# Differential attention: the second map's scaling on GpSimd, difference and transposes one unit later, scores over each map's own 64 partitions

## The chip, the cores and the metric

The kernel runs on 1 core of one Trainium2 chip. The metric is the time of one execution in device microseconds (us); smaller is better. The engines of the core are called here as the profile calls them: PE (TensorE, matmuls; PEld its weight loads), DVE (VectorE), ACT (ScalarE), POOL (GpSimd) and SP (SyncE, which here only issues DMAs).

## The reference, cut to what matters

The kernel computes one inference step of a two-layer trunk with 128 context tokens and 512 latent tokens side by side (640 in all, D_MODEL 1024). Each layer has three token mixers on one input projection (an mLSTM, a latent attention called MLA, and the differential attention), a gated merge of the three and a squared-ReLU MLP. The change is in the differential attention, which has 4 heads with two softmax maps each:

```
q_d = dq.reshape(B, N, H_D, 2, DK_D)          # DK_D = 64, two maps side by side: 128 values a head
k_all, v_all = concat(cache, own)             # latent queries: 128 cached + 512 own keys
def one(qbs):
    p = probs(qbs[0], k)                      # softmax of the first map
    p = p - lam * probs(qbs[1], k2)           # minus lambda times softmax of the second
    return einsum("bhqk,bkhe->bqhe", p, v)
```

## The kernel before, in words

All five engines have a program written out by hand, in fixed order, and they meet at semaphores. Weights come from HBM in 512 KB blocks through a ring of four buffers (SP issues them). POOL splits each block into a rounded part `w_hi` and a remainder `w_lo` (L427, L430), 144 blocks a layer, and PE does three matmuls for each product (L459, L462, L463 in `project`). There are two slots for split blocks, so POOL may split a block only when PE has begun the block before it (`block_used`, L426).

The differential attention stands in each layer between the projections `dq`, `dk`, `dv` and the merge of the MLA branch (`merge_a`). Its input is `q_d` and `k_d` [128 partitions, head, token]: on partitions 0 to 63 lies the head's first map, on 64 to 127 the second. So that a matmul over all 128 partitions gives one map's scores alone, DVE lays out `q_map`: two buffers (in `stage` and `sq`), each with two copies of a head's queries, in which the other map's 64 partitions are zero (memsets L1712, copies L1718 in `lay_out`).

The work of the stage is 20 **units** a layer: 4 heads, and in each 4 tiles of 128 latent queries (640 keys: a *full* unit) and at last the 128 context queries (128 keys: a *late* unit, `LATE`). The functions called `attend` (one on each engine) go through them in a software pipeline. For unit i:

- PE `scores` (L614): for each of the two maps m one PSUM buffer of two banks (`big`, alternating), each of two matmuls with 320 columns (a late unit: one of 128). The trace has two records for every such fp32 matmul, so 8 for a full unit, 2 x 1 x 2 for a late one.
- DVE `maxes` (L1356): the negated row maximum of each map, read from PSUM.
- ACT `exps` (L968): exp with the row sum, from PSUM into `prob_tile`; that frees the PSUM buffer for map m of unit i+1.
- DVE `normalise`: reciprocal of the two row sums (L1364), second map times its factor and -lambda (L1371), then first map times its factor plus the second (L1373); this releases `p_ready`.
- PE `turn` (L628): 5 transposes into the one PSUM tensor `two`; ACT `copyT` (L978) copies them to SBUF; PE `values` (L645, L643): 10 records that multiply with the values. DVE `outputs` (L1382) copies a finished head from PSUM.

The order on PE in step i is scores(i+1), turn(i-1), values(i-2); on DVE maxes(i+1), normalise(i), outputs; on ACT exps(i+1), copyT(i-1). Three pairs of probability tiles are used in turn (`prob_tile`, L349): two in `prob_d`, the third in `t1` and `rs`. The MLA attention uses the same functions with one map and two heads side by side. POOL has nothing to do in the stage: it has split the first block of `merge_a` and waits for PE to begin it.

Of the kernel before, what the change touches and what calls it, by code (L numbers as in the profile page):

```python
# [23 lines left out]
CTX, LAT, PAST = 128, 512, 128  # L24
# [4 lines left out]
P = 128  # L29
# [113 lines left out]
NEG = -1e30  # L143

# [33 lines left out]
def trunk(nc, xT, condT, consts, small_d, past_d, first_d, w_d, yT, o_ckv, o_kr, o_dk, o_dv, o_C, o_m):  # L178
# [3 lines left out]
    with ctx:  # L182
# [39 lines left out]
        q_map = [stage, sq]  # L222
# [64 lines left out]
        neg_max, row_sum = cols[:, 12:16], cols[:, 16:20]  # L287
# [11 lines left out]
        q_map_ready = sem("q_map_ready")  # L299
# [21 lines left out]
        qnope_copied, v_copied = sem("qnope_copied"), sem("v_copied")  # L321
        maxed, exped, p_ready = sem("maxed"), sem("exped"), sem("p_ready")
# [25 lines left out]
        GROUPS = [(0, 0, CTX), (1, CTX, T)]  # L348
        def prob_tile(prob, maps, i, m):  # L349

            return prob[:, maps * (i % 3) + m, :] if i % 3 < 2 else (t1, rs)[m]
# [37 lines left out]
        def _(pool):  # L389
# [45 lines left out]
        def _(pe):  # L435
# [162 lines left out]
            def attend(l, name, maps, side, unit0, set0, q_of, k_of, v_of, heads, prob, probT, beside=None):  # L598
# [3 lines left out]
                def scores(i):  # L602
# [3 lines left out]
                    if maps == 2 and t == 0:  # L606
                        pe.wait_ge(q_map_ready, l * H_D + h + 1)
# [42 lines left out]
                for i in range(-1, n + 2):  # L650
                    if i + 1 < n:
                        scores(i + 1)
                    if beside and 0 <= i:
                        beside(i)
                    if 0 <= i - 1 < n:
                        turn(i - 1)
                    if 0 <= i - 2 and (i - 2) % side == side - 1:
                        if beside and i % 10 == 1:
                            pe.wait_ge(mod_kept, l * MOD_CHUNKS + 3 + (i - 11) // 10)
                        values((i - 2) // side)  # L660

            pe.wait_ge(started, 1)
            for l in range(DEPTH):
# [190 lines left out]
                attend(l, "da", 2, 1, 40, 4, lambda h, m: q_map[h % 2][:, m, :], lambda h, m: k_d[:, h, :],  # L854
# [30 lines left out]
        def _(act):  # L885
# [65 lines left out]
            def attend(l, name, maps, side, unit0, set0, heads, prob, probT, exp0, beside=None):  # L951
                units = attention_units(heads, side)

                def exps(i):
                    h, t = units[i]
                    if i >= 3:
                        act.wait_ge(pT_ready, l * 60 + unit0 + i - 2)
                    for m in range(maps):
                        use = USE[name][maps * i + m]
                        ps, b, _ = buf(use)  # L960
                        col = 2 * (i % 2) + m
# [20 lines left out]
                for i in range(-1, n + 1):  # L982
                    if i >= 1 and maps == 1:
                        copyT(i - 1)
                    if i + 1 < n:
                        exps(i + 1)
                    if i >= 1 and maps == 2:
                        copyT(i - 1)
                    if beside and i >= 0:
                        beside(i)  # L990
# [316 lines left out]
        def _(dve):  # L1307
# [37 lines left out]
            def attend(l, name, maps, side, unit0, set0, heads, prob, exp0, out, lay_out=None, beside=None):  # L1345
                units = attention_units(heads, side)

                def maxes(i):
                    h, t = units[i]
                    for m in range(maps):  # L1350
# [3 lines left out]
                        col = 2 * (i % 2) + m  # L1354
# [4 lines left out]
                def normalise(i):  # L1359
                    h, t = units[i]  # L1360
                    n = CTX if t == LATE else T
                    c0 = 2 * (i % 2)
# [23 lines left out]
                for i in range(-1, n + 3):  # L1386
                    if i + 1 < n:
                        maxes(i + 1)
                        h, t = units[i + 1]
# [4 lines left out]
                    if i >= side + 2 and i % side == 0:  # L1394
                        outputs((i - side - 2) // side)
# [87 lines left out]
            for l in range(DEPTH):  # L1483
# [203 lines left out]
                attend(l, "ma", 1, 2, 0, 0, H_A, prob_a, 0, o_a, None, mods_beside(l))  # L1687
# [21 lines left out]
                for tile in q_map:  # L1709
                    for m in range(2):  # L1710
                        other = 64 * (1 - m)
                        v.memset(tile[other:other + 64, m, :], 0.0)  # L1712

                def lay_out(h):

                    for m in range(2):
                        r = slice(64 * m, 64 * m + 64)
                        v.tensor_copy(q_map[h % 2][r, m, :], q_d[r, h, :])  # L1718
                    dve.drain().then_inc(q_map_ready, 1)
                lay_out(0)  # L1720
                lay_out(1)
# [3 lines left out]
                attend(l, "da", 2, 1, 40, 4, H_D, prob_d, 40, q_d, lay_out)  # L1725
# [268 lines left out]
```

## Time and profile before

| | |
|---|---|
| Time, median of 3 runs | 2758.0 us (2754.29 to 2760.59) |
| The profiled execution's own time | 2755.17 us |
| Its span in the profile | 2753.3 us |
| Busy share of the span | PE 94%, PEld 87%, DVE 43%, ACT 27%, POOL 48% |
| Chain that ended last | PE 85%, DVE 8%, ACT 2% |
| Mean granted TensorE clock | 0.978 of full speed |
| Matmuls of scores, L614 (MLA included), with 96 rows | x288, 89.1 us busy |
| DVE maxima, L1356 (MLA included) | x160, 112.5 us busy |
| POOL's splits, L427 and L430 | x288 each, 556.8 and 742.4 us busy |

A row of a timeline gives the start in us from the span's start, the length of the row, the engine, the line of the kernel and the operation, with the number of instructions merged into it; "[... <-X]" is idle time before it and what ended it. A PE row of several matmuls is longer than their distance to the next row's start, because the last one's pipeline is counted; the distance between starts is what PE spends. The granted clock stands as a share of full speed.

### The profile page before, as it was taken

The page shows a single profiled execution, that of the slowest core. Times are in us where ns is not written, and L with a number is a line of the kernel's source. Part 1 is how long each engine was busy: PE and PEld are TensorE (multiplying, and loading weights), DVE is VectorE, ACT ScalarE, POOL GpSimd, SP SyncE. Part 2 cuts the span into 40 slices and gives each one's busy share as a digit, 9 for nine tenths or more (in the row PEclk, how much of TensorE's full clock was granted, in tenths as well). Part 3 has the DMA queues.
Part 4 walks back from the last instruction along what each step waited for, and adds up shares of the span by engine and source line. Part 5 has one row for each costly group of instructions (what it writes and reads, how often), then busy time and mean ns, then how long its engine had stood idle before and what let it go on. Part 6 is the DMA issues. An engine that isn't in the chain of part 4 may idle for free.

```text
span 2753.3 us, 41706 instructions
## 1 busy us (share of the span) xinstructions
PE 2599.3 (94%) x17328; PEld 2405.0 (87%) x17328; DVE 1184.5 (43%) x1708; ACT 742.3 (27%) x1332; POOL 1329.9 (48%) x604
## 2 busy tenths in 40 slices
PE   4999989999999999999979999898999999999997
PEld 3879986777999899999968799668789998999997
DVE  4434255777224522232554422658752173132233
ACT  2252235215312312021123313351343023021121
POOL 2534540340565566666645255205226665666663
PEclk8999999999999999999999899999999999999999
DMA  6201215430222122222211022242102221222221
GB/s 249 69 16 60 68 58 183 170 129 1 71 75 70 62 77 74 73 77 77 74 57 47 17 74 71 93 169 85 39 27 74 77 70 62 77 70 76 77 75 56
DMA packets 62555, 215.33 MB, mean 78 GB/s; under 512 B 6688, under 2 KB 11168, under 8 KB 62112
## 3 DMA queue, kind: packets, MB, share of 16 engines
q1 hardware_dynamic: 56448, 203.97, 21.8%
q10 hardware_dynamic: 5920, 8.70, 0.9%
q8 instruction: 137, 2.24, 0.3%
q14 instruction: 50, 0.41, 0.0%
HBM read 208.15 MB, written 4.49 MB: 77 GB/s over the span
## 4 chain that ended last, share of the span: by engine, by line
PE 85%; DVE 8%; ACT 2%; DVEq 2%; issue 1%; DMA 1%; ACTq 1%; SPq 1%
PE big L459 22%; PE big L462 22%; PE big L463 22%; PE big L614 4%; PE last_two L645 2%; PE two L628 2%; PE last_two L541 1%; PE big L482 1%; DVE cols L1356 1%; PE two L759 1%; PE big L485 1%; PE big L486 1%; PE last_two L759 1%; DMA first_mod<-in_first 1%; DVE sq L1701 1%
## 5 line engine op out<-in xcount | busy, mean ns | idle before, releaser
L427 POOL TENSOR_TENSOR w_hi<-raw,cst 128x1024 fp32r<-128x1024 f32 x288 | 556.8, 1933 | 1295.4 <-PE big L459 1183.4
L459 PE MATMUL big<-act_hi,w_hi 128*128 128x320 f32 x2784 | 871.0, 313 | 21.6 <-ACT stage L1208 6.5
L462 PE MATMUL big<-act_lo,w_hi 128*128 128x320 f32 x2784 | 864.4, 310 | 0.0
L463 PE MATMUL big<-act_hi,w_lo 128*128 128x320 f32 x2784 | 864.1, 310 | 0.0
L430 POOL TENSOR_TENSOR w_lo<-raw,w_hi 128x1024 fp32r<-128x1024 f32 x288 | 742.4, 2578 | 41.0
L459 PEld LDWEIGHTS big<-act_hi,w_hi 128*128 128x128 f32 x2784 | 526.7, 189 | 32.5 <-issue 29.4
L462 PEld LDWEIGHTS big<-act_lo,w_hi 128*128 128x128 f32 x2784 | 526.9, 189 | 0.9
L463 PEld LDWEIGHTS big<-act_hi,w_lo 128*128 128x128 f32 x2784 | 526.3, 189 | 0.0
L459 PE MATMUL big<-u_hi,w_hi 128*128 128x320 f32 (+1 forms) x1024 | 320.6, 313 | 12.7 <-DVE cols L1793 10.8
L462 PE MATMUL big<-u_lo,w_hi 128*128 128x320 f32 (+1 forms) x1024 | 319.2, 312 | 0.0
L463 PE MATMUL big<-u_hi,w_lo 128*128 128x320 f32 (+1 forms) x1024 | 318.8, 311 | 0.0
L1757 DVE SCALAR_TENSOR_TENSOR x<-big,mods,x 128x128 f32<-128x128 f32 (+2 forms) x240 | 90.8, 434 | 339.3 <-PE big L463 339.3
L1286 ACT ACTIVATE sq<-sq,cols 128x128 f32<-128x128 f32 (+1 forms) x128 | 65.1, 555 | 620.2 <-DVEq L1794 620.2
L459 PEld LDWEIGHTS big<-u_hi,w_hi 128*128 128x128 f32 x1024 | 194.3, 190 | 14.2 <-issue 11.8
L462 PEld LDWEIGHTS big<-u_lo,w_hi 128*128 128x128 f32 x1024 | 195.2, 191 | 0.0
L463 PEld LDWEIGHTS big<-u_hi,w_lo 128*128 128x128 f32 x1024 | 194.4, 190 | 0.0
L1792 DVE TENSOR_TENSOR sq<-big,rs 128x640 f32<-128x640 f32 x64 | 52.8, 824 | 308.7 <-PE big L463 293.2
L1356 DVE TENSOR_REDUCE cols<-big 128x1 f32<-128x640 f32 (+1 forms) x160 | 112.5, 715 | 113.2 <-PE big L614 111.2
L1313 DVE TENSOR_TENSOR act_lo<-stage,act_hi 128x640 fp32r<-128x640 f32 x64 | 118.5, 1852 | 14.4 <-ACT act_hi L1294 6.5
L1332 DVE SCALAR_TENSOR_TENSOR t<-stage,big 128x640 f32<-128x640 f32 x32 | 26.3, 821 | 200.1 <-PE big L463 199.4
L942 ACT ACTIVATE stage<-big 128x640 f32<-128x640 f32 x48 | 33.8, 704 | 288.0 <-PE big L463 288.0
L614 PE MATMUL big<-k_a,q_a 96*128 96x320 f32 (+1 forms) x288 | 89.1, 429 | 4.6 <-DVEq L1685 3.1
(301 smaller groups left out, 3504.3 us busy)
## 6 DMA issues: line engine op xcount, KB each, us to landing
raw<-in_w SPq DMA_DIRECT2D x368, 512.0 KB, 3.5
first_mod<-in_first SPq DMA_DIRECT2D x16, 512.0 KB, 15.7
x<-in_x ACTq DMA_DIRECT2D x1, 2560.0 KB, 12.6
out_y<-x SPq DMA_DIRECT2D x8, 320.0 KB, 2.3
cst<-in_const ACTq DMA_DIRECT2D x1, 1664.0 KB, 10.9
small<-in_small ACTq DMA_DIRECT2D x2, 437.0 KB, 8.9
out_C<-c_new ACTq DMA_DIRECT2D x2, 258.0 KB
v_d<-in_past ACTq DMA_DIRECT2D x2, 256.0 KB, 3.0
```

The lines of the kernel that those rows point to most:

```text
L427: nc.gpsimd.tensor_tensor(w_hi[:, to, :], raw[:, slot, :], ones[:, 0:1].to_broadcast([P, BLK]), ALU.mult)
L430: nc.gpsimd.tensor_tensor(w_lo[:, to, :], raw[:, slot, :], w_hi[:, to, :].bitcast(f32), ALU.subtract).then_inc(split_ready, 1)
L459: first = mm(ps, wh, ah, start=k == 0, stop=False)
L462: mm(ps, wh, al, start=False, stop=False)
L463: last = mm(ps, wl, ah, start=False, stop=k == nk - 1)
L614: last = mm(ps[:, c, 0:n], q_of(h, m)[:, q0:q1], k_of(h, m)[:, k0 + c * n:k0 + c * n + n], start=True, stop=True)
L628: last = nc.tensor.transpose(out, src[:, P * c:P * c + P], ident)
L645: last = mm(one[0][r, P * t:P * t + P], v_of(side * p + g, c + 1), turned, start=c == 0, stop=c == 4)
L1286: f(sq[:, m % 2, a:b], sq[:, m % 2, a:b], ACT.Relu, bias=shift_out[:, m % 2, g:g + 1])
L1313: v.tensor_tensor(lo, src, hi.bitcast(f32), ALU.subtract).then_inc(lo_done, 1)
L1356: v.tensor_reduce(neg_max[:, col:col + 1], src, AX.X if t == LATE else AX.XY, ALU.max, negate=True).then_inc(maxed, 1)
L1757: last = v.scalar_tensor_tensor(x[:, m, o + a:o + z], t[:, h, a:z], mods[:, l, 8 * gate + m, g:g + 1], x[:, m, o + a:o + z], ALU.mult, ALU ...
```

## The change

The differential attention (`maps == 2`) is changed in three ways, the MLA attention keeps its order:

1. **POOL scales the second map.** DVE makes, beside the reciprocal, the factor 1/sum x (-lambda) (one number a partition) and releases `factor_ready`; POOL multiplies the second map's tile with it in `second_maps` and releases `scaled_1`. `second_maps` runs all 20 units of a layer before POOL splits the second block of `merge_a`.
2. **One unit later.** DVE does the difference of unit i-1 after `normalise(i)`; PE transposes unit i-2 and multiplies unit i-3 in step i; ACT copies unit i-2. There are four pairs of probability tiles in place of three (the fourth is `sq`), and four pairs of `neg_max`/`row_sum` columns.
3. **Scores over 64 partitions.** The matmuls read `q_d` and `k_d` on partitions 64m to 64m+63. `q_map`, its memsets, its copies and the semaphore `q_map_ready` are gone.

```
+MLA_LAG, DIFF_LAG = 1, 2
+COPY_FIRST = {1: True, 2: False}
...
-            return prob[:, maps * (i % 3) + m, :] if i % 3 < 2 else (t1, rs)[m]
+            n = i % (LAG[maps] + 2)
+            if n < 2:
+                return prob[:, maps * n + m, :]
+            if maps == 1:
+                return (t1, rs)[n - 2]
+            return (t1, rs)[m] if n == 2 else sq[:, m, :]
...
+            def second_maps(l):
+                for i, (h, t) in enumerate(attention_units(H_D, 1)):
+                    n, c = CTX if t == LATE else T, 2 * (i % 4) + 1
+                    pool.wait_ge(factor_ready, l * 20 + i + 1)
+                    p1 = prob_tile(prob_d, 2, i, 1)[:, 0:n]
+                    nc.gpsimd.tensor_tensor(p1, p1, row_sum[:, c:c + 1].to_broadcast([P, n]), ALU.mult)\
+                        .then_inc(scaled_1, 1)
...
+                if block == FIRST_BLOCK["merge_a"] + 1:
+                    second_maps(l)
...
-                    if maps == 2 and t == 0:
-                        pe.wait_ge(q_map_ready, l * H_D + h + 1)
...
-                for i in range(-1, n + 2):
+                for i in range(-1, n + lag + 1):
                     if i + 1 < n:
                         scores(i + 1)
...
-                    if 0 <= i - 1 < n:
-                        turn(i - 1)
+                    if 0 <= i - lag < n:
+                        turn(i - lag)
+                    j = i - lag - 1
+                    if 0 <= j and j % side == side - 1:
...
+                        values(j // side)
...
-                attend(l, "da", 2, 1, 40, 4, lambda h, m: q_map[h % 2][:, m, :], lambda h, m: k_d[:, h, :],
+                attend(l, "da", 2, 1, 40, 4, lambda h, m: q_d[64 * m:64 * m + 64, h, :],
+                       lambda h, m: k_d[64 * m:64 * m + 64, h, :],
...
-                        p1 = prob_tile(prob, maps, i, 1)[:, 0:n]
-                        v.tensor_scalar(p1, p1, row_sum[:, c0 + 1:c0 + 2], neg_lam, ALU.mult, ALU.mult)
-                        dve.drain()
-                        v.scalar_tensor_tensor(p0, p0, row_sum[:, c0:c0 + 1], p1, ALU.mult, ALU.add)\
+                        v.tensor_tensor(row_sum[:, c0 + 1:c0 + 2], row_sum[:, c0 + 1:c0 + 2], neg_lam, ALU.mult)
+                    dve.drain()
+                    if maps == 2:
+                        dve.drain().then_inc(factor_ready, 1)
+
+                def difference(i):
+                    dve.wait_ge(scaled_1, l * 20 + i + 1)
+                    p0, p1 = (prob_tile(prob, maps, i, m)[:, 0:n] for m in range(2))
+                    v.scalar_tensor_tensor(p0, p0, row_sum[:, c0:c0 + 1], p1, ALU.mult, ALU.add)\
                             .then_inc(p_ready, 1)
...
-                        if maps == 2 and t == LATE and h + 2 < heads:
-                            lay_out(h + 2)
                     if 0 <= i < n:
                         normalise(i)
+                    if maps == 2 and 0 <= i - 1 < n:
+                        difference(i - 1)
```

How the order on PE moves, at the start of the stage in the first layer (`stage`, `sq` and `q_d` hold the queries; `k_d` the keys; `two` takes the transposes, `last_two` the values). Before:

```order
L614 MATMUL big<-k_d,stage 128x320 x12
L628 MATMUL two<-cst,prob_d 128x128 x5
L614 MATMUL big<-k_d,stage 128x320 x4
L628 MATMUL two<-cst,prob_d 128x128 x5
L645 MATMUL last_two<-probT_d,v_d 128x128 x5
L614 MATMUL big<-k_d,stage 128x128 x2
```

After:

```order
L630 MATMUL big<-k_d,q_d 128x320 x16
L644 MATMUL two<-cst,prob_d 128x128 x5
L630 MATMUL big<-k_d,q_d 128x128 x2
L644 MATMUL two<-cst,prob_d 128x128 x5
L661 MATMUL last_two<-probT_d,v_d 128x128 x5
L630 MATMUL big<-k_d,q_d 128x320 x4
```

The scores of four units stand ahead of the first transposes, where there were three, and at the end of the stage one more pair of transposes and values stands behind the last scores.

On DVE, the same place, from the maxima of the third unit on. Before:

```order
L1356 TENSOR_REDUCE cols<-big 128x1 [waits ready_b]
L1356 TENSOR_REDUCE cols<-big 128x1 [waits ready_a]
L1364 RECIPROCAL cols<-cols 128x2 [waits exped]
L1371 TENSOR_SCALAR prob_d<-prob_d,cols 128x640
L1373 SCALAR_TENSOR_TENSOR prob_d<-prob_d,cols 128x640
```

After:

```order
L1377 TENSOR_REDUCE cols<-big 128x1 [waits ready_b]
L1377 TENSOR_REDUCE cols<-big 128x1 [waits ready_a]
L1385 RECIPROCAL cols<-cols 128x2 [waits exped]
L1391 TENSOR_TENSOR cols<-cols 128x1
L1403 SCALAR_TENSOR_TENSOR prob_d<-prob_d,cols 128x640 [waits scaled_1]
```

The pass over 640 columns (L1371) has become one over a single column (L1391), and the difference, now of the unit before, waits for POOL. On POOL, between the split of the first and of the second block of `merge_a` (before, L427 and L430 followed one another there), after:

```order
L448 TENSOR_TENSOR w_lo<-raw,w_hi 128x1024
L420 TENSOR_TENSOR prob_d<-prob_d,cols 128x640 x2
L420 TENSOR_TENSOR rs<-rs,cols 128x640
L420 TENSOR_TENSOR sq<-sq,cols 128x640
L420 TENSOR_TENSOR prob_d<-prob_d,cols 128x128
L420 TENSOR_TENSOR prob_d<-prob_d,cols 128x640
```

20 such products stand between two blocks in each layer, 16 of 640 columns and 4 of 128; the DMAs that wait for a split behind them are those of the ring.

## Rows read from the trace of the kernel before

**Rows 1.** Timeline of PE, first layer; start us, us, engine line op, count [idle before].
```profile
625.25 2.32 PE L614 MATMUL big<-k_d,sq 128*128 128x320 f32 x8
627.40 0.71 PE L628 MATMUL two<-cst,prob_d 128*128 128x128 f32 x5
627.95 1.28 PE L645 MATMUL last_two<-probT_d,v_d 128*128 128x128 f32 x10
629.06 2.32 PE L614 MATMUL big<-k_d,sq 128*128 128x320 f32 x8
...
639.89 0.49 PE L614 MATMUL big<-k_d,sq 128*128 128x128 f32 x2
...
643.54 2.32 PE L614 MATMUL big<-k_d,stage 128*128 128x320 f32 x8
```

**Rows 2.** Timeline, all engines, where the scores of the first layer begin.
```profile
608.14 2.39 PE L614 MATMUL big<-k_d,stage 128*128 128x320 f32 x8 [1.90 <-ACT v_d L1256]
...
609.49 0.83 DVE L1356 TENSOR_REDUCE cols<-big 128x1 f32<-128x640 f32 x1 [3.04 <-PE big L614]
610.35 0.79 ACT L968 ACTIVATE prob_d<-big,cols 128x640 f32<-128x640 f32 x1 [1.87 <-DVE cols L1356]
...
611.29 2.42 PE L614 MATMUL big<-k_d,stage 128*128 128x320 f32 x8 [0.76 <-ACT prob_d L968]
611.42 0.79 ACT L968 ACTIVATE prob_d<-big,cols 128x640 f32<-128x640 f32 x1 [0.19 <-DVE cols L1356]
```

**Rows 3.** Timeline of DVE in one step with two full units.
```profile
652.36 1.57 DVE L1356 TENSOR_REDUCE cols<-big 128x1 f32<-128x640 f32 x2
...
653.84 0.15 DVE L1364 RECIPROCAL cols<-cols 128x2 f32<-128x2 f32 x1
...
654.07 0.61 DVE L1371 TENSOR_SCALAR rs<-rs,cols 128x640 f32<-128x640 f32 x1
...
654.76 0.89 DVE L1373 SCALAR_TENSOR_TENSOR t<-t,cols,rs 128x640 f32<-128x640 f32 x1
...
655.74 0.69 DVE L1382 COPY q_d<-last_two 128x512 f32<-128x512 f32 x1
```

**Rows 4.** Timeline of PE, end of the stage in the first layer.
```profile
676.49 0.49 PE L614 MATMUL big<-k_d,sq 128*128 128x128 f32 x2
...
683.69 0.39 PE L459 MATMUL big<-act_hi,w_hi 128*128 128x320 f32 x1
```

**Rows 5.** Timeline of PE in the mLSTM scores and values, matmuls over 64 and 128 rows.
```profile
151.87 0.92 PE L736 MATMUL big<-qm,km 64*128 64x384 f32 x4
...
152.83 0.39 PE L459 MATMUL big<-act_hi,w_hi 128*128 128x320 f32 x1
...
166.27 0.49 PE L755 MATMUL two<-small,stage 64*128 64x129 f32 x2
166.69 0.94 PE L759 MATMUL two<-vm,ea 128*128 128x129 f32 x6
167.55 0.49 PE L755 MATMUL two<-small,stage 64*128 64x129 f32 x2
```

**Rows 6.** Timeline of POOL and DVE in the rotation of the keys; durations (min/median/max ns) of two lines.
```profile
588.39 2.40 POOL L430 TENSOR_TENSOR w_lo<-raw,w_hi 128x1024 fp32r<-128x1024 f32 x1
...
588.40 2.93 DVE L1704 TENSOR_TENSOR k_d<-t,sq 128x512 f32<-128x512 f32 x1
...
L1704 DVE TENSOR_TENSOR k_d<-t,sq x8: 691/693/2928, 560.6 to 1941.3; 128x512 f32<-128x512 f32 x8
...
L427 POOL TENSOR_TENSOR w_hi<-raw,cst x288: 1886/1894/2642, 22.8 to 2719.6; 128x1024 fp32r<-128x1024 f32 x144
```

**Rows 7.** Timeline: an ACT operation and the POOL operation it releases.
```profile
161.75 1.43 ACT L1088 ACTIVATE stage<-bc_all,small 64x512 f32<-64x512 f32 x2
...
163.26 1.26 POOL L404 TENSOR_TENSOR stage<-stage,qm 128x512 f32<-128x512 f32 x1 [11.76 <-ACT stage L1088]
```

**Rows 8.** Window: stretch, us, busy us of PE, PEld, DVE, ACT, POOL, then PEclk, DMA share, GB/s.
```profile
1924.00:1928.00 4.00, 1.70 (x4) 1.44 (x5) 3.75 (x7) 0.70 (x1) 0.79 (x1) 0.52 0.00 0
```

More of the change, by code:

```diff
@@ L220, in trunk @@
         qm, km = at("qm", [P, 2, T], A0), at("km", [P, 2, T], A0 + 5120)
-        q_map = [stage, sq]
         vm = at("vm", [P, 5, H_M, DV_1], A0 + 10240)
@@ L321, in trunk @@
         qnope_copied, v_copied = sem("qnope_copied"), sem("v_copied")
+        factor_ready, scaled_1 = sem("factor_ready"), sem("scaled_1")
         maxed, exped, p_ready = sem("maxed"), sem("exped"), sem("p_ready")
@@ L649, in attend @@
                 n = len(units)
-                for i in range(-1, n + 2):
+                lag = LAG[maps]
+                for i in range(-1, n + lag + 1):
                     if i + 1 < n:
@@ L654, in attend @@
                         beside(i)
-                    if 0 <= i - 1 < n:
-                        turn(i - 1)
[L657 to L660, printed above, removed]
+                    if 0 <= i - lag < n:
+                        turn(i - lag)
+                    j = i - lag - 1
+                    if 0 <= j and j % side == side - 1:
+                        if beside and j % 10 == 9:
+                            pe.wait_ge(mod_kept, l * MOD_CHUNKS + 3 + j // 10)
+                        values(j // side)
             pe.wait_ge(started, 1)
@@ L955, in exps @@
                     h, t = units[i]
-                    if i >= 3:
-                        act.wait_ge(pT_ready, l * 60 + unit0 + i - 2)
+                    lag = LAG[maps]
+                    if i >= lag + 2:
+                        act.wait_ge(pT_ready, l * 60 + unit0 + i - lag - 1)
                     for m in range(maps):
@@ L960, in exps @@
                         ps, b, _ = buf(use)
[L961 removed]
+                        col = 2 * (i % 4) + m
                         act.wait_ge(maxed, l * 80 + exp0 + maps * i + m + 1)
@@ L981, in attend @@
                 n = len(units)
-                for i in range(-1, n + 1):
-                    if i >= 1 and maps == 1:
-                        copyT(i - 1)
+                lag = LAG[maps]
+                for i in range(-1, n + lag):
+                    if i >= lag and COPY_FIRST[maps]:
+                        copyT(i - lag)
                     if i + 1 < n:
                         exps(i + 1)
-                    if i >= 1 and maps == 2:
-                        copyT(i - 1)
+                    if i >= lag and not COPY_FIRST[maps]:
+                        copyT(i - lag)
                     if beside and i >= 0:
@@ L1343, in merge, with attend @@
                         behind(m)
-            def attend(l, name, maps, side, unit0, set0, heads, prob, exp0, out, lay_out=None, beside=None):
+            def attend(l, name, maps, side, unit0, set0, heads, prob, exp0, out, beside=None):
                 units = attention_units(heads, side)
@@ L1361, in normalise @@
                     n = CTX if t == LATE else T
-                    c0 = 2 * (i % 2)
+                    c0 = 2 * (i % 4)
                     dve.wait_ge(exped, l * 80 + exp0 + maps * (i + 1))
@@ L1385, in attend @@
                 n = len(units)
-                for i in range(-1, n + 3):
+                lag = LAG[maps]
+                for i in range(-1, n + lag + 2):
                     if i + 1 < n:
                         maxes(i + 1)
-                        h, t = units[i + 1]
-                        if maps == 2 and t == LATE and h + 2 < heads:
-                            lay_out(h + 2)
                     if 0 <= i < n:
                         normalise(i)
-                    if i >= side + 2 and i % side == 0:
-                        outputs((i - side - 2) // side)
+                    if maps == 2 and 0 <= i - 1 < n:
+                        difference(i - 1)
+                    j = i - lag - 2
+                    if j >= 0 and j % side == side - 1:
+                        outputs(j // side)
                     if beside and i >= 0:
@@ L1708, in _ @@
                         keep_mod(l + 1, 0, FIRST_CHUNKS[0], one[1][:, 0:256])
[L1709 to L1721, printed above, removed]
                 if l + 1 < DEPTH:
                     keep_mod(l + 1, 1, FIRST_CHUNKS[1], one[1][:, 0:256])
-                attend(l, "da", 2, 1, 40, 4, H_D, prob_d, 40, q_d, lay_out)
+                attend(l, "da", 2, 1, 40, 4, H_D, prob_d, 40, q_d)
                 for h in range(H_D):
```

11 lines of the change are left out of this document (7 added, 4 removed).

## The prediction

> **What bounds the kernel now.** The page's busy shares and its chain name PE as the engine that sets the end, so I read the stage of the differential attention on PE first. In the timeline of PE [rows 1] the reader is to see that full units follow one another with no idle time: scores from 625.25 to 627.40 (2.15 us), transposes 0.55, values 1.11, next scores at 629.06, so 3.81 us a unit. A whole head takes 643.54 - 625.25 = 18.29 us, of which the step with the late unit's scores is 643.54 - 639.89 = 3.65. The first layer's stage lasts from 608.14 [rows 2] to 683.69 [rows 4]: 75.55 us. Two layers are about 150 us of the 2755, and nothing outside them is changed.
>
> Next, the loop through one PSUM buffer, in the timeline of all engines where the stage begins and nothing else is in the way [rows 2]: scores at 608.14, maximum at 609.49, exp at 610.35, next scores into that buffer at 611.29. **3.15 us** is the shortest pitch for one map. The second map's exp starts 1.07 later (611.42), so its buffer is free **4.22 us** after the first map's matmuls start. Last, DVE in a full step [rows 3]: maxima to reciprocal 1.48, reciprocal 0.23, scaling 0.69, difference 0.98 (starts to starts): 3.38 us, below PE's 3.81. So PE is the bound in full steps, and in steps with a late unit it is the loop.
>
> **The change part by part.**
>
> *DVE's scaling goes to POOL.* DVE loses 0.69 and gets a one-column product; the nearest row is the reciprocal, 0.23. A full step is 1.48 + 0.23 + 0.23 + 0.98 = 2.92 us. Since DVE's 3.38 lay beside PE's 3.81, the saving itself is worth nothing. POOL's product reads one tile and one broadcast column, as its first split does: 1.894 us for 1024 columns [rows 6], so an estimated 1.18 for 640. That is shorter than a step, the result is needed a step later, and POOL's next work, the second block of `merge_a`, waited for PE to begin the first in any case. The ring's DMAs wait for that same split, so they do not move: 0. The removed memsets and copies ran on DVE while PE did `dv` or in the late steps; there the transposes wait for ACT's copy: 0.
>
> *64 partitions.* How long is a step's scores now? The mLSTM scores have this form [rows 5]: two fp32 matmuls of 384 columns, one on each half of the partitions, four records. In [rows 1] eight records of 320 columns take 2.15, so 0.27 each; four of 384 would need 0.32 x 4 = 1.29 one behind the other. They began at 151.87, and PE was on the next block at 152.83: 0.96, with a change to 128 rows inside it. The halves ran together. By this a unit's maps need 1.07 us when both buffers are free, and (x + 1.07) when the second comes x later.
>
> *Changes of shape.* A record of 128 columns takes 0.11 (0.55 for five transposes [rows 1]). The two 64-row records at 166.27 took 0.42 and the six 128-row ones behind them 0.86 [rows 5], against 0.22 and 0.66: **0.2 us for each change of shape**. A step now has two, 0.4 us. Taken in full where PE is the bound; the lower bound is 0, if they lie in a wait.
>
> The Trainium skill speaks of the same: "TensorEngine Tiling (Array Packing)", section Key Properties, says that changing the tiling mode drains TensorE, against this change; it gives no duration, and the rows agree that there is a cost.
>
> *A step on PE* is then x + 1.07 + 0.4 + 0.55 + 1.11 = x + 3.13, at least 3.15 by the loop; and the next x is 4.22 less the step's length, since the second buffer comes no earlier. Through a head, from the scores of its first unit with x = 0: 3.15; then x = 1.07, 4.20; then x = 0.02 with the late unit's single transpose, 3.15 by the loop; then x = 1.07 with the late unit's values (0.22), 3.31; then the late scores with x = 0.91, whose transposes wait for ACT's copy as before: 3.65 less the 0.09 that the second exp comes earlier, 3.56. Sum **17.37** against 18.29: **-0.92 a head**. (The same rule with serial scores gives 1.07 + 1.08 + 1.66 = 3.81 for the old step, as measured.)
>
> *The later unit.* Filling: four scores alone at 3.15 each (12.60), then a late step of 3.65: 16.25 until the second head's first scores, against 625.25 - 608.14 = 17.11: -0.86. Two heads in the middle: -1.84. From the fourth head's first scores (643.54 + 18.29 = 661.83) to its last (676.49 [rows 4]) 14.66, now 17.37 - 3.56 = 13.81: -0.85. Emptying: 7.20 (676.49 to 683.69) gets one transposition and one set of values more, +1.66. A layer: -0.86 - 1.84 - 0.85 + 1.66 = **-1.9 us**, both **-3.8 us**.
>
> Who waits for DVE's new wait? Behind the difference stand the next maxima, thus ACT and the scores. POOL's result of a step is ready 1.2 us after the factor, or 2.1 if POOL has first to let DVE's difference (0.89) pass; the difference comes 2.9 after it. No wait in full steps; in late ones some tenths, beside the 3.56.
>
> From the profiled execution's 2755.17 this gives 2751.4. The median of the runs shown lies 2.8 above that execution, so I forecast **2754.2** for a median. About 0.2% (5.5 us) is what a measurement of this kernel can tell from no change. With changes of shape at no cost, a head is 3.15 + 3.80 + 3.15 + 3.15 + 3.65 = 16.90, a layer -3.4 and the sum -6.8: 2748 to 2751, the low end.
>
> **The rivals.**
>
> 1. *POOL takes the port first (slower).* Two operations started at 588.39 on POOL and 588.40 on DVE [rows 6]. POOL's kept its 2.40; DVE's, with two inputs in SBUF, took 2.93 where it needs 0.69: it stood until POOL's was over. In the new order POOL's product and DVE's difference are both free to start when `factor_ready` is given, in every step. If POOL's starts first, the difference is put off by 1.18 and DVE's step is 2.92 + 1.18 = 4.10, longer than PE's. A head: two such full steps, one of them with an output copy of 0.69 [rows 3]; one with a short product, 3.3; one with a short difference, 3.6; the late one 3.56: 19.4, +1.1. Filling about +1.2, the last head +1.2, emptying +2.8: +7.4 a layer, +15: **2773**. It decides who is first by some hundredths. POOL's operation started 163.26 - (161.75 + 1.43) = 0.08 after the ACT operation that released it [rows 7]; DVE goes on 0.08 after its reciprocal, behind a drain (653.84 + 0.15 to 654.07 [rows 3]), and POOL's 0.08 counts from a release that lies behind that same drain. So DVE is more likely first, by little. The Trainium skill, "SBUF — State Buffer", section "SBUF: two separate sides", calls it an exclusive lock for a whole instruction that goes to whoever starts first; the two starts 0.01 apart agree.
>
> 2. *The halves do not run together here.* In [rows 5] the second half stood behind two records; here it stands behind four and a wait of its own. If matmuls only start in order, the second map starts when the first one's last record has: x is at least 0.80, and a head is 3.93 + 3.93 + 3.49 + 3.15 + 3.72 = 18.22, a layer +0.6, in all +1: **2759**. With no overlap at all x is 1.07: 4.20 + 4.20 + 3.76 + 3.31 + 3.56 = 19.03, a layer +3.1, in all +6: **2764**. The Trainium skill, "TensorE: Matmul & The Clock Gate", Part 3, states that matmuls keep program order in start and end; the 0.96 of the rows is shorter than that rule allows, so they speak against it here.
>
> 3. *The clock.* After a stretch with PE idle the granted clock was 0.52 of full speed in the window from 1924 [rows 8]. Filling the pipeline is now one step longer, with PE's scores at a third to two thirds of each. If the clock falls to its lower level there, ten us of PE work at twice its length less the waits it fills give +3 to +8: about **2761**.
>
> 4. *More than I count*: PE's remaining waits in the late steps go too. Three of them a layer at 1 us: -10 in all, **2748**.
>
> **How the numbers follow.** Forecast 0.50, with a spread of 3 us about -3.8: 0.22 of it falls under -5.5 and 0.28 within. Rival 1 0.24, all slower. Rival 2 0.15: 0.09 within, 0.06 slower. Rival 3 0.05, slower. Rival 4 0.06, faster. So faster 0.28, same 0.37, slower 0.35. The range runs from 2748 to rival 1 at 2773; the forecast's own range is 2748 to 2758.
>
> **What would show it.** Full steps on PE alternating about 3.2 and 4.2 us, a head at 17.4; the first two records of both maps starting together where x = 0; 0.2 us at each change of shape; POOL's product of 1.2 us starting behind DVE's difference, which stays at 0.89. Differences of 2 us on DVE would show rival 1, serial records with heads of 18.2 to 19 rival 2, PEclk under 1.00 near the stage's start in both layers rival 3. I am wrong in kind if a head is longer than 18.29, or if the stages' lengths change by more than the kernel's time does.

## The result and the profile after

The changed kernel takes **2784.57 us** (median of 4 runs, 2780.06 to 2789.15) against 2756.14 for the kernel before beside it (2753.28 to 2760.59): ratio 1.010, 95% interval 1.0076 to 1.0124. It is slower by about 28 us. Forecast was 2754.2, with 2773 as the upper end. The profile below is of the slowest of the four executions, 2789.15 us.

Three lines of the page of the changed kernel: busy shares, the chain that ended last, and DVE's maxima (busy us, mean ns | idle before, releaser). They answer to the table of the kernel before.

```profile
PE 2626.4 (94%) x17328; PEld 2419.9 (87%) x17328; DVE 1180.6 (42%) x1684; ACT 742.7 (27%) x1332; POOL 1370.7 (49%) x644
...
PE 85%; DVE 8%; DVEq 2%; ACT 2%; issue 1%; DMA 1%; ACTq 1%; SPq 1%
...
L1377 DVE TENSOR_REDUCE cols<-big 128x1 f32<-128x640 f32 (+1 forms) x160 | 112.0, 715 | 132.0 <-PE big L630 130.0
```

They say little: the same PE share, nearly the same chain, and 19 us more of DVE idle ahead of the maxima (113.2 before, 132.0 now). The stages say it. The profiled execution reached the first layer's stage 7.4 us later than the profiled one of before, in code that is the same in both and where the granted clock fell at other moments; so I measure each stage from its own first scores. Both ends of the first one, in the timeline of PE:

```profile
615.55 1.35 PE L630 MATMUL big<-k_d,q_d 64*128 64x320 f32 x8 [1.90 <-ACT v_d L1277]
...
704.25 0.39 PE L477 MATMUL big<-act_hi,w_hi 128*128 128x320 f32 x1
```

704.25 - 615.55 = 88.70 us, against 75.55 [rows 2, 4]. The second layer's, by the same two landmarks, is 90.05 us against 77.38. Together +25.8 us, of the 33.9 us that lie between the two profiled spans. Of the other 8.1 us, 7.4 are the time lost ahead of the first stage, in code that did not change. The medians lie 28.4 us apart.

**Where in the stage.** The third head in the timeline of PE, to set beside [rows 1]:

```profile
657.99 1.78 PE L630 MATMUL big<-k_d,q_d 64*128 64x320 f32 x8
...
661.66 2.34 PE L630 MATMUL big<-k_d,q_d 64*128 64x320 f32 x8
...
665.74 1.80 PE L630 MATMUL big<-k_d,q_d 64*128 64x320 f32 x8
...
668.98 2.34 PE L630 MATMUL big<-k_d,q_d 64*128 64x320 f32 x8
...
673.02 0.48 PE L630 MATMUL big<-k_d,q_d 64*128 64x128 f32 x2 [0.79 <-ACT prob_d L988]
...
675.17 0.77 PE L644 MATMUL two<-cst,sq 128*128 128x128 f32 x5 [0.66 <-DVE sq L1403]
676.05 2.48 PE L661 MATMUL last_two<-probT_d,v_d 128*128 128x128 f32 x10
678.45 1.79 PE L630 MATMUL big<-k_d,q_d 64*128 64x320 f32 x8
```

The head takes 678.45 - 657.99 = 20.46 us, where it took 18.29 and the forecast was 17.37. Step by step 3.67, 4.08, 3.24, 4.04 and 5.43, against a forecast of 3.15, 4.20, 3.15, 3.31 and 3.56. The fourth and the fifth are the farthest off, and the fifth shows two reasons: the transposes wait for `sq` by the difference on DVE (L1403), and then ten records of values need 678.45 - 676.05 = 2.40 us in place of 1.11. The granted clock was 1.00 in the window from 672 to 676, in which PE was busy for 1.97 of 4 us, and 0.58 in the next:

```profile
672.00:676.00 4.00, 1.97 (x12) 1.16 (x10) 3.67 (x6) 2.48 (x5) 1.25 (x1) 1.00 0.02 4
676.00:680.00 4.00, 3.95 (x18) 3.23 (x18) 2.74 (x6) 1.62 (x5) 1.25 (x1) 0.58 0.00 0
```

**DVE and POOL in one step**, from the timeline of all engines:

```profile
627.30 0.15 DVE L1385 RECIPROCAL cols<-cols 128x2 f32<-128x2 f32 x1
...
627.53 0.16 DVE L1391 TENSOR_TENSOR cols<-cols 128x1 f32<-128x1 f32 x1
627.85 1.25 POOL L420 TENSOR_TENSOR prob_d<-prob_d,cols 128x640 f32<-128x640 f32 x1 [3.08 <-DVEq L1394]
627.87 1.91 DVE L1403 SCALAR_TENSOR_TENSOR prob_d<-prob_d,cols 128x640 f32<-128x640 f32 x1 [0.18 <-issue]
```

POOL's product starts at 627.85, DVE's difference at 627.87: 0.02 us too late. It takes 1.91 us instead of 0.89 [rows 3], that is 1.23 until POOL's product has ended and 0.68 more. It is no accident: of the 40 units of both layers, 38 have a difference beside the product (the first of each layer has none), and in all 38 POOL starts 0.01 or 0.02 us ahead. Here are the durations (min/median/max ns) of the two lines for the tile `prob_d`:

```profile
L1403 DVE SCALAR_TENSOR_TENSOR prob_d<-prob_d,cols x20: 1069/1911/1924, 627.9 to 2062.3; 128x640 f32<-128x640 f32 x16, 128x128 f32<-128x128 f32 x4
...
L420 POOL TENSOR_TENSOR prob_d<-prob_d,cols x20: 398/1252/1252, 623.5 to 2058.7; 128x640 f32<-128x640 f32 x16, 128x128 f32<-128x128 f32 x4
```

**The clock.** Windows of 6 us from the stage's start (us, busy us of PE, PEld, DVE, ACT, POOL, then PEclk, DMA share, GB/s):

```profile
612.00:618.00 6.00, 3.00 (x17) 1.91 (x15) 1.28 (x3) 2.67 (x4) 0.00 (x0) 1.00 0.39 131
618.00:624.00 6.00, 4.47 (x10) 2.81 (x11) 2.33 (x5) 3.30 (x8) 0.48 (x1) 0.50 0.00 0
624.00:630.00 6.00, 5.16 (x14) 3.29 (x14) 3.90 (x6) 1.77 (x4) 2.02 (x2) 0.50 0.00 1
630.00:636.00 6.00, 5.32 (x20) 3.76 (x19) 5.23 (x10) 3.65 (x10) 2.09 (x2) 0.50 0.00 0
636.00:642.00 6.00, 5.93 (x34) 4.65 (x34) 3.50 (x6) 2.06 (x5) 0.81 (x2) 0.80 0.00 0
```

The granted clock is at its lower level (0.50 of full, 1.2 GHz), from 618 until after 636, while PE waits between the scores of the filling. In the second layer it stays there for 24 us. In the kernel before it was 1.00 through the first layer's filling, and fell once, shortly, at the start of the second layer's:

```profile
1958.00:1962.00 4.00, 3.91 (x8) 2.34 (x8) 0.82 (x1) 1.13 (x3) 0.00 (x0) 0.57 0.18 68
1962.00:1966.00 4.00, 3.44 (x11) 1.84 (x11) 2.26 (x3) 1.96 (x6) 0.00 (x0) 1.00 0.00 0
```

So a fall there is not new; that it lasts is. Filling took 22.02 us in place of 17.11 in the first layer, and 22.73 in place of 18.92 in the second.

### The profile page after: what moved, and what is told of

Its sections match the earlier page's. It is cut to its first block, busy times and chain, and to the rows that moved or that the text cites. A ratio compares the mean times of both kernels' runs of the same rounds, so it can differ in the third digit from the quotient of the medians.

```text
span 2787.2 us, 41745 instructions
## 1 busy us (share of the span) xinstructions
PE 2626.4 (94%) x17328; PEld 2419.9 (87%) x17328; DVE 1180.6 (42%) x1684; ACT 742.7 (27%) x1332; POOL 1370.7 (49%) x644
## 4 chain that ended last, share of the span: by engine, by line
PE 85%; DVE 8%; DVEq 2%; ACT 2%; issue 1%; DMA 1%; ACTq 1%; SPq 1%
PE big L477 22%; PE big L480 21%; PE big L481 21%; PE big L630 4%; PE last_two L661 2%; PE two L644 2%; PE last_two L559 1%; PE big L500 1%; PE big L503 1%; PE big L504 1%; PE two L777 1%; DVE cols L1377 1%; PE last_two L777 1%; DMA first_mod<-in_first 1%; DVE sq L1732 1%
## 5 line engine op out<-in xcount | busy, mean ns | idle before, releaser
L477 PE MATMUL big<-u_hi,w_hi 128*128 128x320 f32 (+1 forms) x1024 | 320.7, 313 | 12.8 <-DVE cols L1811 10.8
L1377 DVE TENSOR_REDUCE cols<-big 128x1 f32<-128x640 f32 (+1 forms) x160 | 112.0, 715 | 132.0 <-PE big L630 130.0
L630 PE MATMUL big<-k_d,q_d 64*128 64x320 f32 (+1 forms) x288 | 82.1, 531 | 21.0 <-ACT prob_d L988 11.5
## 6 DMA issues: line engine op xcount, KB each, us to landing
cst<-in_const ACTq DMA_DIRECT2D x1, 1664.0 KB, 10.7
```

What stands on the lines that cost most here:

```text
L477: first = mm(ps, wh, ah, start=k == 0, stop=False)
L630: last = mm(ps[:, c, 0:n], q_of(h, m)[:, q0:q1], k_of(h, m)[:, k0 + c * n:k0 + c * n + n], start=True, stop=True)
L1377: v.tensor_reduce(neg_max[:, col:col + 1], src, AX.X if t == LATE else AX.XY, ALU.max, negate=True).then_inc(maxed, 1)
```

## The experiments

All lengths below are from the profiled execution of each kernel, from the first scores of the stage to the first matmul of the merge behind it. "Fill" is until the second head's first scores, "head" the second and third, "end" from the last head's late scores on. Each row is one execution. The kernel before needs 1.8 us more in its second layer than in its first with the same instructions (the short fall of the clock), so a difference of that size between two rows is not shown by them alone. The first four experiments ran on one chip and the last four on another, each time with the kernel before beside them (2758.83 and 2757.79 us).

| kernel | scores over | one unit later | second map scaled | first layer | second layer | fill | head | end |
|---|---|---|---|---|---|---|---|---|
| before | 128 | no | DVE | 75.55 | 77.38 | 17.11 / 18.92 | 18.30 | 7.20 |
| the change | 64 | yes | POOL, first | 88.70 | 90.05 | 22.02 / 22.73 | 20.5 | 10.8 / 10.9 |
| e1_dve_scales | 64 | yes | DVE | 80.62 | 81.91 | 21.43 / 21.58 | 17.7 to 19.0 | 9.44 |
| e5_factor_later | 64 | yes | POOL, second | 79.99 | 80.44 | 21.43 / 21.58 | 17.54 (one 17.92) | 9.3 to 10.0 |
| e2_full_rows | 128 | yes | POOL, first | 86.11 | 88.57 | 19.26 / 20.69 | 20.5 to 20.8 | 10.7 / 11.2 |
| e3_rows_alone | 64 | no | DVE | 76.16 | 78.03 | 19.22 / 21.09 | 17.83 | 7.08 |
| e8_rows_busy | 64 | no | DVE | 74.07 | 74.08 | 17.13 / 17.13 | 17.83 | 7.08 |
| e7_later_busy | 64 | yes | POOL, second | 76.87 | 74.68 | 18.02 / 16.51 | 17.54 | 9.3 to 10.0 |
| e4_later_alone | 128 | yes | DVE | 79.13 | 79.72 | 17.93 / 18.40 | 18.1 to 18.7 | 9.3 to 10.0 |
| e6_pool_full_rows | 128 | yes | POOL, second | 76.99 | 77.72 | 17.80 / 18.15 | 17.82 | 9.4 to 9.8 |

**e1_dve_scales: POOL's part undone.**

```
-                if block == FIRST_BLOCK["merge_a"] + 1:
-                    second_maps(l)
-                        v.tensor_tensor(row_sum[:, c0 + 1:c0 + 2], row_sum[:, c0 + 1:c0 + 2], neg_lam, ALU.mult)
-                    dve.drain()
-                    if maps == 2:
-                        dve.drain().then_inc(factor_ready, 1)
+                        p1 = prob_tile(prob, maps, i, 1)[:, 0:n]
+                        v.tensor_scalar(p1, p1, row_sum[:, c0 + 1:c0 + 2], neg_lam, ALU.mult, ALU.mult)
+                    dve.drain()
-                    dve.wait_ge(scaled_1, l * 20 + i + 1)
```

Expected: 

> The change with the scaling of the second map back on DVE (as before), one unit later and over 64 partitions. Theory L (POOL's product takes the port and the difference on DVE lasts 1.92 us instead of 0.88): the difference is back at 0.88, DVE needs 3.4 us a full step, and the heads shrink from 20.4 to about 18 us. Theory C (the scores over 64 partitions, or the longer filling, let the clock fall to 1.2 GHz at the start of each stage): the filling still takes 22 us in place of 17 and the granted clock is still 0.50 there. If both hold, a stage is 80 to 83 us (88.7 and 90.1 in the change, 75.6 and 77.4 before). If L alone, 75; if C alone, 88.

Measured: 2770.04 us against 2758.83 (ratio 1.0036, 1.0021 to 1.0051), stages of 80.62 and 81.91. The difference is back at 0.88, heads at 17.7 to 18.1 (one of 19.0, with a fall of the clock in it), the filling still 21.5 at half clock. Both theories hold, side by side: the stages are 8.1 us shorter than the change's, each, and still 5.1 and 4.5 longer than before.

**e5_factor_later: the order of two starts turned round.** `factor_ready` of unit i is released behind the difference of unit i-1; POOL's product then starts 1.13 us after the factor is made, where it was 0.16.

```
                     dve.drain()
-                    if maps == 2:
-                        dve.drain().then_inc(factor_ready, 1)
...
                         difference(i - 1)
+                    if maps == 2 and 0 <= i < n:
+                        dve.drain().then_inc(factor_ready, 1)
```

Expected: 

> The change, but factor_ready is released behind the difference of the unit before, so that DVE's difference has the port first and POOL's product runs beside the maxima. Theory L: the difference takes 0.88 us, POOL's product 1.25, full steps on PE average 3.7, and the late steps lose the wait for the difference: a stage is 8 to 11 us shorter than the change's, 78 to 81. Rival: the length of 1.92 is not the order of the starts but comes of reading a tile that POOL has written; then it stays at 1.92 and nothing changes.

Measured: 2769.22 us against 2758.83 (1.0038, 1.0023 to 1.0053). Durations of the two lines:

```profile
L1401 DVE SCALAR_TENSOR_TENSOR prob_d<-prob_d,cols x20: 350/884/886, 623.4 to 2044.0; 128x640 f32<-128x640 f32 x16, 128x128 f32<-128x128 f32 x4
...
L420 POOL TENSOR_TENSOR prob_d<-prob_d,cols x20: 398/1252/1254, 619.1 to 2042.5; 128x640 f32<-128x640 f32 x16, 128x128 f32<-128x128 f32 x4
```

DVE's difference is 0.88, POOL's product 1.25, and the tile that POOL wrote is as fast to read as any other; the rival falls. One step on DVE shows more:

```profile
653.94 0.16 DVE L1391 TENSOR_TENSOR cols<-cols 128x1 f32<-128x1 f32 x1 [0.43 <-issue]
654.18 0.88 DVE L1401 SCALAR_TENSOR_TENSOR prob_d<-prob_d,cols 128x640 f32<-128x640 f32 x1
```

With one drain between them in place of two, the difference starts 654.18 - 654.10 = 0.08 us after the factor, where it was 0.18 in the change. POOL's product now runs beside the maxima, which read PSUM: they last 0.83 us at most, as they do without it. PE's timeline of one head:

```profile
650.51 1.35 PE L630 MATMUL big<-k_d,q_d 64*128 64x320 f32 x8
...
653.75 2.34 PE L630 MATMUL big<-k_d,q_d 64*128 64x320 f32 x8
...
657.83 1.61 PE L630 MATMUL big<-k_d,q_d 64*128 64x320 f32 x8
...
661.07 2.34 PE L630 MATMUL big<-k_d,q_d 64*128 64x320 f32 x8 [0.25 <-ACT prob_d L988]
...
664.31 0.48 PE L630 MATMUL big<-k_d,q_d 64*128 64x128 f32 x2
...
668.05 1.35 PE L630 MATMUL big<-k_d,q_d 64*128 64x320 f32 x8
```

Steps of 3.24, 4.08, 3.24, 3.24 and 3.74: **17.54 us, where the forecast had 3.15, 4.20, 3.15, 3.31, 3.56 and 17.37**. This is close to the forecast's head, alternation included. The stages are 8.7 and 9.6 us shorter than the change's. So the order of two starts 0.02 us apart costs 18 us of the kernel; the medians beside the kernel before agree (+28.4 in the change, +10.4 here). The filling is nearly as slow as in the change, at the same low clock:

```profile
616.00:620.00 4.00, 3.17 (x10) 1.82 (x8) 1.88 (x4) 1.77 (x4) 0.86 (x1) 0.50 0.00 0
...
628.00:632.00 4.00, 3.88 (x17) 3.47 (x17) 2.65 (x6) 2.60 (x8) 2.06 (x2) 0.50 0.00 0
```

**e2_full_rows: the 64 partitions undone**, POOL first and one unit later as in the change.

```
-                attend(l, "da", 2, 1, 40, 4, lambda h, m: q_d[64 * m:64 * m + 64, h, :],
-                       lambda h, m: k_d[64 * m:64 * m + 64, h, :],
+                attend(l, "da", 2, 1, 40, 4, lambda h, m: q_map[h % 2][:, m, :], lambda h, m: k_d[:, h, :],
...
+        q_map = [stage, at("q_map1", [P, 2, T], A0 + 70656)]
```

Expected: 

> The change with the scores over all 128 partitions again (q_map in stage and in a buffer of its own behind the others), POOL scaling and one unit later. Theory C by the 64 rows: the clock stays at full speed through the filling, which takes about 19 us, and a stage is 80 to 83 us, all that is left being the lock. Rival, the longer filling alone lowers the clock: 0.50 at the start of the stages as in the change, and 88 to 92 us a stage.

Measured: 2777.99 us against 2758.83 (1.0074, 1.0053 to 1.0096), stages of 86.11 and 88.57, longer than I expected. Heads of 20.5 to 20.8 us show that the difference behind POOL's product costs as much with scores over 128 partitions. Its difference, as in the change:

```profile
L1406 DVE SCALAR_TENSOR_TENSOR prob_d<-prob_d,cols x20: 1069/1913/1924, 621.3 to 2048.7; 128x640 f32<-128x640 f32 x16, 128x128 f32<-128x128 f32 x4
```

The filling is 19.3 and 20.7. In the first layer the clock falls once, shortly, near its end (0.86 and 0.71 in the windows from 624 to 632), in the second layer twice (0.57 from 1968, 0.67 from 1984), in place of 20 and 24 us at 0.50. So the 64 partitions make the fall last, as theory C says, but the filling with one more unit is not free of falls without them.

**e3_rows_alone: the 64 partitions alone**, on top of the kernel before (`q_map` and its work gone, one unit later and POOL not taken over).

```
-                attend(l, "da", 2, 1, 40, 4, lambda h, m: q_map[h % 2][:, m, :], lambda h, m: k_d[:, h, :],
+                attend(l, "da", 2, 1, 40, 4, lambda h, m: q_d[64 * m:64 * m + 64, h, :],
+                       lambda h, m: k_d[64 * m:64 * m + 64, h, :],
```

Expected: 

> The kernel before with the scores over 64 partitions, nothing else: DVE scales, no unit later. Theory C by the 64 rows: the clock falls to 0.50 at the start of the stages, the filling is 3 to 5 us longer and a stage is 79 to 82 us. Rival (the longer filling or the lock made PE idle): the clock stays, full steps on PE average 3.7 instead of 3.8, and a stage is 74 to 76 us.

Measured: 2756.0 us against 2758.83 (0.9992, 0.9976 to 1.0007): no difference. The stages are 76.16 and 78.03, below the 79 to 82 of theory C; the clock does fall as it says, but the filling lost 2.1 us in each layer and not 3 to 5. Heads gained 0.47 us each (17.83 for 18.30). The first scores of the stage and the next ones, in the timeline of all engines:

```profile
608.36 1.35 PE L610 MATMUL big<-k_d,q_d 64*128 64x320 f32 x8 [1.90 <-ACT v_d L1253]
...
611.51 3.50 PE L610 MATMUL big<-k_d,q_d 64*128 64x320 f32 x8 [1.79 <-ACT prob_d L965]
```

Eight records that took 2.39 over 128 partitions [rows 2] take 1.35 here, so the two maps ran together entirely. Then PE is idle for 1.79 us, and the next eight take 3.50. Windows of 4 us from 608 on:

```profile
608.00:612.00 4.00, 1.84 (x9) 1.29 (x10) 1.56 (x2) 2.02 (x5) 0.00 (x0) 0.78 0.17 66
612.00:616.00 4.00, 3.17 (x9) 1.70 (x8) 1.72 (x3) 1.44 (x5) 0.00 (x0) 0.50 0.00 0
616.00:620.00 4.00, 4.00 (x12) 2.60 (x13) 2.94 (x4) 1.55 (x4) 0.00 (x0) 0.50 0.00 2
620.00:624.00 4.00, 4.00 (x25) 2.90 (x24) 3.66 (x8) 2.65 (x8) 0.00 (x0) 0.94 0.00 0
```

The clock is at 0.50 for 10 us in the first layer and 17 us in the second. A step in which PE does not wait, at the end of the first layer's filling, shows what the changes of shape cost:

```profile
626.37 1.28 PE L641 MATMUL last_two<-probT_d,v_d 128*128 128x128 f32 x10
627.58 1.35 PE L610 MATMUL big<-k_d,q_d 64*128 64x320 f32 x8
628.86 0.77 PE L624 MATMUL two<-cst,prob_d 128*128 128x128 f32 x5
629.47 1.28 PE L641 MATMUL last_two<-probT_d,v_d 128*128 128x128 f32 x10
```

Values 1.21, scores 1.28, transposes 0.61, from start to start: 3.10 us, where 1.11, 1.07 (four records in place of eight) and 0.55 would be 2.73. Two changes of shape cost 0.37.

**e8_rows_busy: the same with work in PE's gaps.** Four matmuls of 256 columns ahead of the stage, three behind the first scores, one behind the second; they write to a PSUM bank that the values overwrite, and nobody reads them.

```
+                def keep_busy(k):
+                    for _ in range(k):
+                        mm(one[0][:, 0:256], ident, cst[:, 0:256], start=True, stop=True)
+                if maps == 2:
+                    pe.wait_ge(o_copied, l * 16 + 8)
+                    keep_busy(4)
                 for i in range(-1, n + 2):
                     if i + 1 < n:
                         scores(i + 1)
+                    if maps == 2:
+                        keep_busy({-1: 3, 0: 1}.get(i, 0))
```

Expected: 

> The kernel before with the scores over 64 partitions (as in e3_rows_alone), and eight matmuls of 256 columns over all 128 partitions, whose result nobody reads, in PE's gaps ahead of and between the first scores of each stage. Theory C (the clock falls because the halves that run together leave PE idle in the filling): the granted clock stays at 1.00 through the filling of both layers, which takes 17 us instead of 19.2 and 21.1; heads stay at 17.83 us, the stage is 74 us, 2 to 4 us shorter than in e3_rows_alone, and the kernel is about 5 us faster than before. Rival (matmuls over 64 partitions get less clock whatever stands beside them): the clock is 0.50 again and the stage stays at 76 and 78 us or grows by the added work.

Measured: 2753.9 us against 2757.79 (ratio 0.9984, 0.9974 to 0.9994), faster than the kernel before by 0.16%; stages of **74.07 and 74.08 us**. PE's timeline (L647 are the added matmuls) and the windows:

```profile
608.69 1.99 PE L647 MATMUL last_two<-cst 128*128 128x256 f32 x8 [0.35 <-DVEq L1444]
610.62 1.35 PE L610 MATMUL big<-k_d,q_d 64*128 64x320 f32 x8
611.90 1.56 PE L647 MATMUL last_two<-cst 128*128 128x256 f32 x6
613.79 2.34 PE L610 MATMUL big<-k_d,q_d 64*128 64x320 f32 x8 [0.33 <-ACT prob_d L974]
```

```profile
608.00:612.00 4.00, 3.65 (x20) 2.35 (x18) 0.18 (x2) 2.43 (x3) 0.00 (x0) 1.00 0.31 123
612.00:616.00 4.00, 3.67 (x14) 2.29 (x14) 2.38 (x3) 1.77 (x4) 0.00 (x0) 1.00 0.06 22
616.00:620.00 4.00, 3.79 (x16) 2.16 (x15) 3.57 (x6) 2.10 (x5) 0.00 (x0) 1.00 0.01 2
```

The clock stays at 1.00, the filling is 17.13 in both layers, and the stage is 2.1 and 4.0 us shorter than without the added work. Four of the added matmuls stand ahead of the first scores and so outside the stage, mostly in a wait that PE has there anyway; from the last matmul of the projections to the merge the gain is 1.7 and 4.0 us (78.67 and 80.54 in e3_rows_alone, 76.97 and 76.50 here). Theory C holds: matmuls over 64 partitions get the full clock when PE has work beside them. How much of the 0.16% is due to the added work the whole kernels do not tell: the interval of e3_rows_alone overlaps this one.

**e7_later_busy: e5_factor_later with nine such matmuls** (one more, behind the third scores).

Expected: 

> The change with factor_ready behind the difference (e5_factor_later) and nine such matmuls in the gaps of the filling. Theory C: clock 1.00, filling 16.3 us instead of 21.5, heads 17.5, end 9, a stage of 75 us in place of 80. Rival: the clock is 0.50 again, 80 us or more.

Measured: 2759.26 us against 2757.79 (1.0006, 0.9995 to 1.0017): no difference from before. The second layer's stage is 74.68 with the clock at 1.00 throughout and a filling of 16.51 (forecast 16.25). In the first layer the clock fell once late in the filling (0.59 in the window from 624 to 628) and once at the end (0.81 and 0.76 from 676 to 684): 76.87. This is the whole change with POOL's product second and most of the low clock taken away. Where the clock held, it stands 0.6 us above the same stage of e8_rows_busy (74.07), which has neither the later unit nor POOL.

**e4_later_alone: the later unit alone**, DVE scaling and scores over 128 partitions.

Expected: 

> The kernel before with the difference, transposes and copies one unit later and nothing else: DVE scales, scores over all 128 partitions. It gives the price of the later unit. Forecast's step: heads 17.8 to 18.3 us, end 8.9 in place of 7.2, filling 16.3 to 17 if the clock stays: 76 us a stage. If the longer filling by itself lowers the clock: 19 to 21 us of filling and 0.50 in its windows.

Measured, one run: 2762.14 us; stages of 79.13 and 79.72. The end is 9.3 to 10.0 us where it was 7.2, heads 18.1 to 18.7, the filling 17.9 and 18.4 with short falls of the clock. The 76 us expected for the stage was too low by 3 to 4. In this one execution the later unit by itself costs 3.6 and 2.3 us a layer, most of it at the end, and gains nothing.

**e6_pool_full_rows: the same with POOL second.**

Expected: 

> As e4_later_alone, with the second map scaled on POOL and factor_ready behind the difference. If POOL's product costs nothing once it starts second, heads are as long as in e4_later_alone or up to 0.3 us shorter, and DVE's difference lasts 0.88. Rival (POOL beside DVE costs in another way): heads of 19 us or more.

Measured, one run: 2761.36 us; stages of 76.99 and 77.72. Heads are 17.82 us, 0.3 to 0.9 shorter than in e4_later_alone and 0.48 shorter than before. Released second, POOL's product is a gain in the heads, more than I expected; the end (9.4 to 9.8) takes it back.

## Why the prediction was wrong

The two stages grew by 88.70 + 90.05 - 75.55 - 77.38 = **25.8 us**. The experiments divide it:

- **POOL first: +18.3 us** (178.75 in the change less 160.43 in e5_factor_later). *The step that failed* is "So DVE is more likely first, by little". POOL's start, a drain and 0.08 us behind it, was read rightly: 0.16 after the one-column product. What I took for DVE was 0.08 us, read from a gap with one drain in it. In the changed kernel a second drain stands there and carries the release, and the difference starts 0.18 us after the product's end (627.69 to 627.87). The diff has both drains. With one drain between them, in e5_factor_later, the gap is 0.08 again. A kernel whose first drain carries the release, and which has no second, was not run. The mechanism and its price were worked out as rival 1, which had 0.24. Its +15 us counts from the kernel before; from the forecast it is 18.6, and 18.3 is what was measured. The sum is right partly by luck, since its parts are not: between e5_factor_later and the change the heads grew by 2.9 us and not 2.0, and the filling by 0.6 and 1.2 and not 2.0, as it was slow already. In the heads, PE's longer wait in each late step is followed by a low clock (0.57 to 0.72 in the 4 us behind it, in six of six), which rival 1 did not have.
- **The clock in the filling: +8.9 us** (160.43 less 151.55 in e7_later_busy; 8.6 if the added matmuls ahead of the stage are counted). The medians beside the kernel before agree: +10.4 us and +1.5 us. Rival 3 named place and size (+3 to +8) and got 0.05. The forecast's filling of 16.25 us was worked out at full clock throughout, though the same sum made PE idle for half of each of its steps. That was the second failed step: the saving on PE (two maps in the time of one) was booked where PE is the bound, and what it does where PE is not was left to a rival. Rivals 1 and 3 came true together, which no case of mine had, so the time lies outside the range.
- **The rest: -1.4 us** (151.55 less 152.93; -1.1 with the added matmuls), forecast -3.8. Either sum has one layer with a fall of the clock in it. Of the layers without, 74.68 in e7_later_busy against 75.55 before is -0.9, where the forecast had -1.9.

Point by point, for that rest:

- *The halves run together*: right. Eight records in 1.35 us from the start of the first to the end of the last, behind four records of the first map. Rival 2 falls. The rule of the Trainium skill ("TensorE: Matmul & The Clock Gate", Part 3) that matmuls keep program order in their starts does not fit this: by it the second map could have started only 0.80 us after the first, and the unit could not have been done in 1.35. [Rows 5] spoke against it less than I wrote: it gives 0.32 + 0.64 = 0.96 there, as measured, until a change of shape is added.
- *0.2 us for each change of shape*: right. Two changes cost 0.37 us in the step shown for e3_rows_alone, and the head of 17.54 lies far above the 16.9 that I had worked out with free changes.
- *A head*: 17.37 forecast, 17.54 in e5_factor_later and e7_later_busy at full clock.
- *The filling*: 16.25 forecast, 16.51 where the clock held.
- *Emptying*: 8.86 forecast, 9.3 to 10.0 measured in all kernels that run one unit later, except the two with POOL first (10.7 to 11.2). It was mis-sized by 0.5 to 1.1 us a layer: the last transposes still wait in turn for ACT's copies (0.48 and 0.63 us in e5_factor_later).
- *DVE's saving is worth nothing*: not quite. e6_pool_full_rows against e4_later_alone has heads 0.3 to 0.9 us shorter, e5_factor_later against e1_dve_scales 0.15.
- *The later unit* was booked at -0.86 in the filling and +1.66 at the end. Alone, in one execution, it adds 2.1 and 2.8 us at the end and does not shorten the first layer's filling (17.93 against 17.11).

What stays open: why the clock fell in the first layer of e7_later_busy and not in the second, and in the second layer of the kernel before and not in the first, with the same instructions each time. The moments at which it falls differ from execution to execution also ahead of the stage, and the runs don't settle it.

## What to carry to other kernels

When work moves from DVE to POOL, release it so that DVE's next operation with two inputs in SBUF is already running, and let operations that read PSUM stand beside POOL's, as the maxima do here without loss: moving one release behind one operation was worth 18 us. Before you place two starts by a gap read from an old trace, count the drains in the new code. When a change makes PE faster, look where PE already waits; there the saving turns into idle time and may cost the clock. A scheme that runs one unit deeper must be paid for at the ends of each stage; here 20 units did not earn it back.

## What the runs showed of the hardware that I had not expected

- Two maps in separate halves of the partitions overlap completely although four records of the first (and a wait) stand ahead of the second: 1.35 us for eight records over 64 partitions, 2.39 over 128.
- Of two operations behind one DVE drain, one on POOL that it releases and DVE's own next one, POOL's started 0.01 or 0.02 us ahead in 38 of 38 units. DVE's took 1.91 us in place of 0.88, that is until POOL's 1.25 us were over and 0.68 more; beside a product of 0.40 us it took 1.07.
- Where the first scores over 64 partitions took 1.35 us and PE then stood for 1.8, the granted clock was 0.50 within some 4 us of the stage's start and stayed there for 10 and 17 us (e3_rows_alone), with one unit more for 20 us and longer. Over 128 partitions (2.39 us and 0.76 idle) it fell once in two layers, and shortly. Some 3.4 us of matmuls that nobody reads, an estimate from 16 records 0.21 us apart, kept it at 1.00 in both layers.
